# First scores between the value projections, two weight jobs exchanged, and cross-attention's last exponentials moved up, in a one-core decoder layer

## The reference, cut to what matters

```
h = rms_norm(x, norm_mix)
z = h @ w_in
oa = moba_attention(qa, ka, va, bias_a) @ w_oa           # 8 heads of 64
ob = dsa_attention(qb, kb, vb, q_idx, k_idx, w_idx, bias_b) @ w_ob   # 8 heads of 64
x = x + (sigmoid(z_ga) * oa + sigmoid(z_gb) * ob) @ w_out
x = x + memory_cross_attention(rms_norm(x, norm_x), rms_norm(mem, mem_norm), wq_x, wk_x, wv_x, wo_x)
x = x + hier_moe(rms_norm(x, norm_moe), w_group, b_group, w_router, b_router, w1, w3, w2)
return rms_norm(x, final_norm)
```

## Time and profile before

| what | value |
|---|---|
| median of 3 runs | 707.66 us (706.98 to 707.76) |
| the profiled execution's own time | 707.0 us |
| its span | 705.2 us |
| chain that ended last, by engine | PE 49%, DMA 43%, ACT 3%, DVE 3% |
| PE busy, DVE busy, ACT busy | 515.7 us, 201.5 us, 145.1 us |
| bytes moved by DMA | 244.21 MB |

### The profile page before, as it was taken

The page is one execution under the profiler, slowest core; times in us unless marked ns, Lnnn a source line. Parts: engine busy times, 40 slices in busy tenths (PEclk is TensorE's granted clock), DMA queues, the critical chain, the costliest instruction groups (busy, mean ns, idle before and its releaser), DMA issues.

```text
span 705.2 us, 8763 instructions
## 1 busy us (share of the span) xinstructions
PE 515.7 (73%) x3815; PEld 326.1 (46%) x3815; DVE 201.5 (29%) x368; ACT 145.1 (21%) x250; POOL 16.5 (2%) x28
## 2 busy tenths in 40 slices
PE   6999899999999888855945673473584557347483
PEld 5899799898998663321411131141141114114121
DVE  3697645478765440100100000010010001001002
ACT  6564445354434441000000000000000000000002
POOL 1200000001001000000000000000000000000001
PEclk9999999999999999887887797796788779779688
DMA  9899233606499898999999999999999999999991
GB/s 294 240 352 374 102 120 120 239 1 214 151 353 355 338 398 325 429 427 428 426 429 428 426 427 427 431 427 427 426 428 429 429 427 427 427 427 429 419 394 79
DMA packets 48089, 244.21 MB, mean 346 GB/s; under 512 B 8936, under 2 KB 18352, under 8 KB 37296
## 3 DMA queue, kind: packets, MB, share of 16 engines
q1 hardware_dynamic: 48048, 243.62, 85.7%
HBM read 242.53 MB, written 4.22 MB: 350 GB/s over the span
## 4 chain that ended last, share of the span: by engine, by line
PE 49%; DMA 43%; ACT 3%; DVE 3%; issue 2%; SPq 1%; POOL 0%; POOLq 0%; PEldq 0%; DVEq 0%; ACTq 0%
PE ps L640 15%; DMA slots_own<-in_w 12%; DMA slots_late<-in_w 12%; PE ps L933 10%; DMA attn_data<-in_w 8%; PE ps L659 7%; PE ps L938 6%; DMA slot_mixed<-in_w 4%; DMA slot_spare<-in_w 4%; PE ps L618 1%; PE ps L947 1%; DMA slots_own<-in_w_in 1%; PE ps L1005 1%; PE ps L685 1%; SPq L505 1%
## 5 line engine op out<-in xcount | busy, mean ns | idle before, releaser
L933 PE MATMUL ps<-slots_late,x_sb 128*32 128x512 f32 x336 | 88.9, 686 | 38.7 <-DMA slot_mixed<-in_w 16.1
L933 PE MATMUL ps<-attn_data,x_sb 128*32 128x512 f32 x176 | 72.0, 708 | 21.7 <-DMA slots_own<-in_w 21.7
L1584 DVE TENSOR_TENSOR bqT<-ps,bqT 128x512 f32<-128x512 f32 x8 | 5.5, 692 | 236.2 <-ACT bqT L1248 236.2
L938 PE MATMUL ps<-slots_own,vb 128*32 128x512 f32 x192 | 54.7, 727 | 23.8 <-DMA slot_spare<-in_w 8.8
L410 DVE TENSOR_TENSOR w_low<-slots_own,w_high 128x2048 fp32r<-128x2048 f32 (+1 forms) x32 | 64.7, 2022 | 24.2 <-ACT w_high L1061 24.0
L1245 ACT ACTIVATE vb<-ps 128x256 f32<-128x256 f32 x8 | 3.1, 384 | 309.6 <-PE ps L975 309.6
L933 PE MATMUL ps<-slot_spare,x_sb 128*32 128x512 f32 x112 | 51.4, 664 | 14.5 <-DMA attn_data<-in_w 14.5
L933 PE MATMUL ps<-slots_own,x_sb 128*32 128x512 f32 x240 | 55.2, 665 | 5.9 <-DMA slot_spare<-in_w 3.2
L1061 ACT ACTIVATE w_high<-slots_own 128x2048 fp32r<-128x2048 f32 (+1 forms) x32 | 54.2, 1694 | 21.6 <-PE ps L659 10.8
L640 PE MATMUL ps<-h_high,w_high 128*128 128x256 f32 x224 | 56.3, 291 | 0.0
L933 PEld LDWEIGHTS ps<-slots_late,x_sb 128*32 128x32 f32 x336 | 22.6, 124 | 71.7 <-issue 71.7
(11 more groups left out here) (263 smaller groups left out, 929.9 us busy)
## 6 DMA issues: line engine op xcount, KB each, us to landing
slots_own<-in_w SPq DMA_DIRECT2D x27, 2048.0 KB, 34.2
slots_late<-in_w SPq DMA_DIRECT2D x26, 2048.0 KB, 34.9
attn_data<-in_w SPq DMA_DIRECT2D x17, 2048.0 KB, 34.5
slot_last<-in_w SPq DMA_DIRECT2D x9, 2048.0 KB, 36.4
slot_spare<-in_w SPq DMA_DIRECT2D x9, 2048.0 KB, 34.1
slots_own<-in_w_in SPq DMA_DIRECT2D x8, 2048.0 KB, 11.7
slot_mixed<-in_w SPq DMA_DIRECT2D x8, 2048.0 KB, 32.6
slots_own<-in_w_out SPq DMA_DIRECT2D x2, 2048.0 KB, 7.8
```

The lines of the kernel that those rows point to most:

```text
L933: return pe.matmul(ps[SLOTS * e:SLOTS * e + SLOTS, 4 + matrix, :], xeT[:, k, SLOTS * e:SLOTS * e + SLOTS], w, start=(k == 0), stop=(k == K ...
L938: return pe.matmul(ps[SLOTS * e:SLOTS * e + SLOTS, 4 + c, :], actT[:, f, SLOTS * e:SLOTS * e + SLOTS], w, start=(f == 0), stop=(f == FC - ...
L1584: dve.tensor_tensor(act_sb, ps[:, 5, :].rearrange("p (q f) -> p f q", f=FC), silu_sb.rearrange("p (f q) -> p f q", f=FC), ALU.mult).then_i ...
```

## The change

Four things are changed. (1) In the indexer, DVE writes the keys `ikT` ahead of the head weights `iwT`, with a semaphore of their own, and PE waits for this one before `index_logits(0)`; it waits for the head weights behind it. (2) `scores(0)` stands between the two value projections `av0` and `av1` instead of behind them, and `logits(0)`, `exps(0)` and `normalise(0)` stand there too. (3) `oa1` and `gb2` are exchanged in `JOBS` and `SPLITS`, and the jobs of steps 6 to 8 are shared out differently; `oa3` stands behind step 8. (4) In cross-attention ACT runs `cross_exp(3)` and the copy of `vm` before `cross_copy(0)`, and DVE runs `cross_normalise(3)` before `cross_copy(1)`. No work is added or removed, and SP's list of DMAs is the same.

```
-STEP_JOBS = [(None, None), ("ga0", "ga1"), ("ga2", "ga3"), ("bq0", "bq1"), (None, "gb0"), ("gb1", "oa0"),
-             ("gb2", "oa1"), ("gb3", "oa2"), ("oa3", None)]
+STEP_JOBS = [("av0", "av1"), ("ga0", "ga1"), ("ga2", "ga3"), ("bq0", "bq1"), (None, "gb0"), ("gb1", "oa0"),
+             ("oa1", "gb2"), (None, "gb3"), (None, "oa2")]
...
             job_evacuated(pe, "iq")
-            job_evacuated(pe, "ikw")
+            pe.wait_ge(keys_set, 1)
             index_logits(0)
             pe.wait_ge(biasrow_set, 1)
+            job_evacuated(pe, "ikw")
...
-            split_rows("av0", h)
-            split_rows("av1", h)
-            pe.wait_ge(h_low_set, 8)
...
+            pe.wait_ge(h_low_set, 8)
+            split_rows("av0", h)
+            scores(0)
+            split_rows("av1", h)
+            for n in range(1, 9):
...
+            split_columns("oa3", oA)
             pe.wait_ge(o_split, 8)
...
+            for i in range(2):
+                copy_job(f"av{i}", av[:, :, 256 * i:256 * i + 256], by_rows)
+                after(f"av{i}")
+                if i == 0:
+                    exps(0)
...
             cross_exp(2)
-            cross_copy(0)
             cross_exp(3)
             copy_job("vm", vm.rearrange("p a b -> p (a b)"))
+            cross_copy(0)
             cross_copy(2)
...
-            dve.tensor_scalar(iwT, o[0:IDX_HEADS, T:2 * T], IDX_HEADS ** -0.5 * IDX_DIM ** -0.5, None, ALU.mult)
-            evacuates(dve.tensor_copy(ikT[:], o[:, 0:T]), "ikw")
+            dve.tensor_copy(ikT[:], o[:, 0:T]).then_inc(keys_set, 1)
+            evacuates(dve.tensor_scalar(iwT, o[0:IDX_HEADS, T:2 * T], IDX_HEADS ** -0.5 * IDX_DIM ** -0.5, None,
+                                        ALU.mult), "ikw")
...
+            logits(0)
+            after("av0")
+            normalise(0)
+            after("av1")
+            for n in range(1, 9):
...
             cross_normalise(2)
+            cross_normalise(3)
             cross_copy(1)
-            cross_normalise(3)
             cross_copy(3)
```

More of the change, by code:

```diff
@@ L98 @@
         + [f"ga{i}" for i in range(4)]
-        + ["bq0", "bq1", "kb0", "kb1", "vb0", "vb1", "gb0", "gb1", "oa0", "gb2", "oa1", "gb3", "oa2", "oa3"]
+        + ["bq0", "bq1", "kb0", "kb1", "vb0", "vb1", "gb0", "gb1", "oa0", "oa1", "gb2", "gb3", "oa2", "oa3"]
         + [f"ob{i}" for i in range(4)] + ["km"]
@@ L115 @@
 SPLITS = (["iq", "ikw", "ckv", "aq0", "aq1", "ak0", "ak1", "av0", "av1"] + [f"ga{i}" for i in range(4)]
-          + ["bq0", "bq1", "gb0", "gb1", "oa0", "gb2", "oa1", "gb3", "oa2", "oa3"]
+          + ["bq0", "bq1", "gb0", "gb1", "oa0", "oa1", "gb2", "gb3", "oa2", "oa3"]
           + [f"ob{i}" for i in range(4)] + ["km"] + [f"out{i}" for i in range(4)] + ["qx", "vm"])
-STEP_JOBS = [(None, None), ("ga0", "ga1"), ("ga2", "ga3"), ("bq0", "bq1"), (None, "gb0"), ("gb1", "oa0"),
-             ("gb2", "oa1"), ("gb3", "oa2"), ("oa3", None)]
+STEP_JOBS = [("av0", "av1"), ("ga0", "ga1"), ("ga2", "ga3"), ("bq0", "bq1"), (None, "gb0"), ("gb1", "oa0"),
+             ("oa1", "gb2"), (None, "gb3"), (None, "oa2")]
 POOL_LOW = ()
@@ L331, in decoder_layer @@
         ikw_in = sem("ikw_in")
-        iw_turned = sem("iw_turned")
+        iw_turned, keys_set = sem("iw_turned"), sem("keys_set")
         chunk_asked = sem("chunk_asked")
@@ L804, in gate_or_a @@
                 split_columns(name, oA if name[:2] == "oa" else h)
-            for n in range(9):
+            pe.wait_ge(h_low_set, 8)
[3 more added lines that the diff above has]
+            for n in range(1, 9):
                 if n == 4:
@@ L810, in _ @@
                 gate_or_a(ahead)
-                if n >= 1:
-                    turn_probs(n - 1)
+                turn_probs(n - 1)
                 if n < 8:
@@ L815, in _ @@
                 gate_or_a(between)
-                if n >= 1:
-                    weigh(n - 1)
+                weigh(n - 1)
+            split_columns("oa3", oA)
             pe.wait_ge(o_split, 8)
@@ L1124, in _ @@
                     evacuates(m, "ckvT")
-            for i in range(2):
-                copy_job(f"av{i}", av[:, :, 256 * i:256 * i + 256], by_rows)
-                after(f"av{i}")
             def exps(n):
@@ L1175, in _ @@
                     after(ahead)
-                if n >= 1:
-                    copy_probT(n - 1)
+                copy_probT(n - 1)
                 if n < 8:
                     exps(n)
-                if between:
-                    evacuate_job(between)
-                if n >= 1:
-                    copy_o(n - 1)
-                if between:
-                    after(between)
+                evacuate_job(between)
+                copy_o(n - 1)
+                after(between)
+            after("oa3")
             for i in range(4):
@@ L1368, in _ @@
             then(dve.tensor_scalar(unpicked[:], score[:], TAKEN / 2, NEG, ALU.is_gt, ALU.mult))
-            after("av0")
-            after("av1")
             def logits(n):
@@ L1437, in _ @@
                 evacuate_a(between)
-                if n >= 1:
-                    split_o(n - 1)
-                if between:
-                    after(between)
+                split_o(n - 1)
+                after(between)
+            evacuate_a("oa3")
+            after("oa3")
             dve.wait_ge(gates_set, 2)
```

## The result

| | before | after |
|---|---|---|
| median of the runs, us | 707.61 (706.98 to 707.76, 4 runs) | 700.65 (699.48 to 702.16, 4 runs) |
| profiled execution, us | 707.0 | 700.77 |
| its span, us | 705.2 | 699.0 |

The ratio is 0.989, with an interval from 0.9861 to 0.992: faster by 1.1%.

What follows compares the result with a forecast made beforehand. PE was taken to bound the kernel up to the twelfth expert unit's issue at 267.71 us, the weight stream behind it. 0.34 + 4.89 + 0.07 + 1.42 = 6.7 us gave 700.3, plus 0.7 for the median: 701.0, range 699.6 to 703.4.

Steps and rivals of the forecast that it cites:

- Keys: Indexer: with the keys written first, PE starts its first score matmul 0.34 us sooner.
- First scores: Step 1, ga0 to ga2: scores between the value projections gain 4.89 us, a 3.13 pause plus 1.76 of slow matmuls.
- The cover of 6 us: Step 0: probabilities ready near 71.3 us, PE asks for them at 77.4, so six us of cover.
- the bias: Load for step 0's logits: landed at 63.5 us, wanted at about 65.5, so 2 us to spare.
- Exchanged jobs: Steps 6 to 8: new pauses of 2.3 us against 2.4 removed, gain 0.07.
- Cross-attention: Head 3's transposes can start at 237.46 us instead of 238.88: gain 1.42 us.
- One for one: What PE's list gains before the twelfth expert unit's issue at 267.71 us comes off the end in full.
- the dry stretch: DMA queue nearly empty from 266 to 268 us; it would shrink by 1.4 us, less than the 2 seen.
- The sum of 6.7: Whole kernel: gains of 0.34, 4.89, 0.07 and 1.42 us add up to 6.7 us.
- the clock did not fall at steps 7 and 8: Rival: the new pauses at step 7 or 8 bring the clock down, costing 1.8 us: 702.7 us, chance 0.10.
- the weight stream would swallow the gain: Rival: the expert weight stream is the bound and nothing comes through: 707.7 us, chance 0.04.

Runs made afterwards that it cites:

- keys_back: The changed kernel with the keys' copy again behind the head weights' scaling on DVE: 702.66 us (one execution).
- jobs_back: The changed kernel with gb2, oa1, gb3, oa2 and oa3 back in their old places: 701.66 us, ratio 0.9901.
- pool_low: The changed kernel with the low part of gb2's weights written by POOL instead of DVE: 700.59 us, ratio 0.9901.
- cross_back: The changed kernel with the old order of ACT's and DVE's work in cross-attention: 701.83 us (one execution).
- the filler: 22 unused 128x512 matmuls added to the changed kernel in PE's wait for the last expert step's second matrix: 704.17 us, ratio 0.9965.
- gates_ahead: The changed kernel with gb0 to gb3 ahead in steps 5 to 8, oa0 in step 8, oa1 to oa3 behind weigh(7): 702.48 us, ratio 0.9911.
- gates_copy: gates_ahead with ACT's copy of the transposed probabilities ahead of the weights' high part instead of behind it: 698.25 us, ratio 0.9874.

## Why the prediction was right

The time, 701.0 forecast and 700.65 measured, was right, and so was the cause. That the two lie within 0.35 us is in part luck: the sum gave 700.3 for the profiled execution, which took 700.77, and 0.7 was added for the median, which came 0.12 below that execution. Term by term:

- **Keys**, 0.34: the pause fell from 0.93 to 0.61 us, 0.32, and came back with keys_back.
- **First scores**, 4.89: 4.88 in the comparison. `ga2` was forecast at 85.6 and began at 85.00, 0.6 of which is the earlier start. The cover of 6 us was there, the bias was no bound. But the split of the term, pause plus 1.76 us of low clock, is less solid than its agreement: the pause is the same in every kernel that has it (3.13, 3.14), the fall behind it cost 1.76 us once and 2.6 to 2.8 once. A price taken from one execution should have had an upper bound; 5.95 was seen.
- **Exchanged jobs**, 0.07, as new pauses of 0.1, 1.3 and 0.93 against 2.4 removed: the pauses measured 0.1, 1.18 and 0.98, the gain 0.17, and 0.29 in jobs_back. The working along DVE's list held: the bottleneck at step 7 was `split_o` behind the low parts, as pool_low bears out.
- **Cross-attention**, 1.42: 1.45 in the comparison, 1.36 in cross_back.
- **One for one**: the distance from the twelfth unit to the last load is 396.84 us against 396.87 before, so the 7.4 us of lead arrived in full at the last load. But the dry stretch did not shrink by 1.4 us, as worked out from the units that `vm` releases. The queue's last work ahead of it is the eleventh unit, and that moved with the twelfth (12.31 us ahead of it before, 12.30 after). The bound on the gain was looked for in the wrong row; it did not bind.
- **The sum of 6.7** stood for the whole span; up to the last load 6.8 us were gained by the terms (0.32 and 6.50). The step that was missing is the one behind it: I had taken the tail behind the last load as constant. It ranges from 40.3 to 42.5 us (42.59 where the filler overran), mostly with the clock around the last weights' landing. It took 1.2 us here, and the earlier start gave 0.6 back.
- **The rivals**: the clock did not fall at steps 7 and 8, as pauses of 1.18 and 0.98 us did nothing to it, nor did 1.55 and 1.35 in gates_ahead. That the weight stream would swallow the gain is refuted by the distance of 396.84. gates_copy, another change to the order of the engines' work ahead of the stream, gained 3 us more in the same way.

## What to carry to other kernels

Where a stream bounds the long part of a kernel but runs dry at its start, every microsecond of the critical engine ahead of that point came off the end here; so find the dry stretch first, and then the critical engine's pauses ahead of it. Price a pause of TensorE by its length and by what its clock does behind it: here pauses of 1 to 1.5 us in the attention steps cost their length, and one of 3.1 us cost 4.9 in one kernel and 6.0 in another. When work is rearranged so that one wait goes, look at what stands in each helper engine's queue ahead of the result that is needed next: the same order of jobs was 0.4 us worse or 3.1 us better by one swap on ScalarE.

## What the runs showed of the hardware

- A fall of the clock behind the same pause has no fixed length: over 80 to 86 us the granted clock was 0.72 in one kernel and 0.50 in another, and the cost 1.8 and 2.8 us. Two waits of 1.69 and 0.78 us, the same in all kernels, were followed by a slow block in four executions of 14.
- In the tail, waits of 1.68 to 2.00 us left the next block at 1.92 us (six executions); waits of 2.37 to 2.82 us were followed by 2.94 to 3.61 us for the same block (five executions).
- Filling a pause with unused matmuls avoided the fall behind it: three of them in 3.1 us gave 2.6 us, seven, which overran the pause, gave nothing. A 128x512 matmul of f32 operands takes 0.87 us at full clock, so their number has to be worked out from a measured row.
- A VectorE operation with both inputs in SBUF, beside a GpSimd operation, ended 0.82 us behind that one's end and took 2.47 us instead of 0.96. The low part itself took 4.60 us on GpSimd and 2.29 on VectorE.
- The start scatters: the first index score matmul came between 25.01 and 26.49 us in kernels whose work ahead of it is the same but for the 0.32 us of the keys. That alone is 0.2% of the time, so parts of under 1 us can be told apart by a distance inside the trace and not by medians of four runs.
